# A 256-token decoder trunk on one core: two first product units interleaved by contraction tile, and transposes in two groups instead of four

## The reference

```python
for layer in range(2):
    xn = rms_norm(h, norm_mix_g[layer])
    proj = xn @ (ab_w_in, cd_w_in)[layer]
    # layer 0: causal pooling over windows 2..16, and differential attention with 6 heads
    # layer 1: gated causal convolution of width 31, and causal attention with 6 heads
    h = h + concatenate([branch_1, branch_2]) @ (ab_w_out, cd_w_out)[layer]
    hn = rms_norm(h, norm_ffn_g[layer])
    h = h + (silu(hn @ w_gate[layer]) * (hn @ w_up[layer])) @ w_down[layer]   # 1024 -> 2816 -> 1024
out = rms_norm(h, norm_final_g)
```

## Time and profile before

| what | us |
|---|---|
| median of three runs | 566.34 |
| time of the profiled execution | 566.4 |
| its span, first to last instruction | 564.1 |
| TensorE busy in the span | 556.9 (99%) |
| VectorE busy | 461.9 (82%) |
| ScalarE busy | 324.3 (57%) |
| memory read, mean rate | 104.11 MB, 186 GB/s |

### The profile page before, as it was taken

One profiled execution on the slowest core, in us unless ns is written; L12 is line 12 of the kernel. 1 busy time (PEld: TensorE's weight loads), 2 busy tenths in 40 slices (PEclk: granted clock), 3 DMA queues, 4 the chain that ended last, 5 costly groups with the idle time before them and its releaser, 6 DMA issues.

```text
span 564.1 us, 7600 instructions
## 1 busy us (share of the span) xinstructions
PE 556.9 (99%) x2949; PEld 475.1 (84%) x2949; DVE 461.9 (82%) x571; ACT 324.3 (57%) x454; POOL 15.5 (3%) x55
## 2 busy tenths in 40 slices
PE   8999999999999999999999999999999999999995
PEld 7899978888888888888888888888888888888884
DVE  5679996776988789897797998977779887798875
ACT  6686864654564555556576356546475545555543
POOL 1200001000000000000000000000000000000000
PEclk9999999999999999999999999999999999999999
DMA  8975644455627394467479622445744464926431
GB/s 297 353 298 164 217 149 145 154 195 180 223 76 243 104 314 159 145 228 255 156 242 315 226 76 74 161 146 164 273 164 140 150 223 150 304 85 215 144 112 74
DMA packets 30419, 105.65 MB, mean 187 GB/s; under 512 B 3376, under 2 KB 4272, under 8 KB 30384
## 3 DMA queue, kind: packets, MB, share of 16 engines
q1 hardware_dynamic: 30240, 105.04, 54.3%
q10 hardware_dynamic: 144, 0.14, 0.1%
HBM read 104.11 MB, written 1.05 MB: 186 GB/s over the span
## 4 chain that ended last, share of the span: by engine, by line
PE 97%; DMA 1%; issue 1%; DVE 1%; SPq 0%; ACT 0%; POOLq 0%; POOL 0%; DVEq 0%
PE bank L1748 20%; PE bank L1746 20%; PE bank L1747 20%; PE bank L2179 13%; PE bank L2182 7%; PE bank L1844 4%; PE bank L1847 2%; PE bank L1791 1%; PE bank L1795 1%; PE bank L1798 1%; PE bank L1816 1%; DMA raw<-in_slabs 1%; PE bank L1936 1%; PE bank L2224 1%; PE bank L1962 0%
## 5 line engine op out<-in xcount | busy, mean ns | idle before, releaser
L1046 DVE TENSOR_TENSOR w_lo<-raw,w_hi 128x2048 fp32r<-128x2048 f32 (+2 forms) x92 | 204.8, 2228 | 35.7 <-ACT w_hi L574 35.7
L574 ACT ACTIVATE w_hi<-raw 128x2048 fp32r<-128x2048 f32 (+2 forms) x83 | 153.7, 1862 | 28.6 <-DMA raw<-in_slabs 26.4
L1746 PE MATMUL bank<-w_lo,yT_hi 128*128 128x512 f32 (+1 forms) x242 | 96.1, 397 | 0.0
L1748 PE MATMUL bank<-w_hi,yT_lo 128*128 128x512 f32 (+1 forms) x242 | 94.1, 389 | 0.0
L1747 PE MATMUL bank<-w_hi,yT_hi 128*128 128x512 f32 (+1 forms) x242 | 94.0, 388 | 0.0
L2179 PE MATMUL bank<-xT,w_hi 128*128 128x512 f32 x320 | 80.5, 393 | 0.0
L2179 PEld LDWEIGHTS bank<-xT,w_hi 128*128 128x128 f32 x320 | 57.8, 189 | 10.6
L1746 PE MATMUL bank<-w_lo,xT 128*128 128x512 f32 (+1 forms) x160 | 61.9, 387 | 0.0
L1748 PE MATMUL bank<-w_hi,xT 128*128 128x512 f32 (+1 forms) x160 | 60.8, 380 | 0.0
L1747 PE MATMUL bank<-w_hi,xT 128*128 128x512 f32 (+1 forms) x160 | 60.6, 379 | 0.0
L1748 PEld LDWEIGHTS bank<-w_hi,yT_lo 128*128 128x128 f32 x242 | 45.4, 188 | 9.6
(11 more groups left out here) (229 smaller groups left out, 840.8 us busy)
## 6 DMA issues: line engine op xcount, KB each, us to landing
raw<-in_slabs SPq DMA_DIRECT2D x170, 512.0 KB, 4.7
spare<-in_slabs SPq DMA_DIRECT2D x16, 512.0 KB, 5.3
raw<-in_slabs SPq DMA_DIRECT2D x6, 256.0 KB, 6.1
h<-in_x SPq DMA_DIRECT2D x2, 512.0 KB, 8.6
gain<-in_norm_ffn_g SPq DMA_DIRECT2D x2, 512.0 KB, 7.2
raw<-in_slabs SPq DMA_DIRECT2D x4, 128.0 KB, 5.5
h<-in_x_cols SPq DMA_DIRECT2D x1, 512.0 KB, 6.3
gain<-in_norm_mix_g SPq DMA_DIRECT2D x1, 512.0 KB, 5.7
```

Of the source, the lines that this page charges most:

```text
L574: A(w_hi[:, s % SLOTS, c], raw_of(r, c), ACT.Copy).then_inc(hi_ready, 1)
L1046: V.tensor_tensor(w_lo[:, s % SLOTS, c], raw_of(preps[s][0], c), w_hi[:, s % SLOTS, c].bitcast(F32), ALU.subtract).then_inc(lo_ready, 1)
L1746: T.matmul(o, st_hi, mv_lo, start=first, stop=False)
L1748: return T.matmul(o, st_lo, mv_hi, start=False, stop=last)
```

## The change

There are two edits. The first interleaves the two first units: for each contraction tile `k`, TensorE does the six matmuls of unit 0 and then the six of unit 1. Slabs are renumbered to match (0: unit 0, tiles 0 to 3; 1: unit 1, tiles 0 to 3; 2: unit 0, tiles 4 to 7; 3: unit 1, tiles 4 to 7). SyncE loads the parts of slabs 0 and 1 alternately, with the token columns between them, and the last four token tiles after both slabs. ScalarE and VectorE split both slabs' parts of a tile before the next token tile; the first halves of slabs 2 and 3 are split between the token tiles 4 and 5 to 7. The copies of banks 4 and 5 wait for the third release of a slab instead of the second.

The second edit moves the turns of a seven-product unit: `turn(0)` and `turn(1)` stand together after the first contraction tile of product `t4`, and `turn(2)` and `turn(3)` together between the two blocks of the last down product. ScalarE's and VectorE's steps are reordered for it: `seven_gate(a, 1)` comes before the split of the next down slab, the split of the next up slab before `seven_hi(a, 0)`.

```diff
         SEVEN_HALF, SEVEN_CHUNK, SEVEN_TURN_BANK = (0, 1, 1, 0), (1, 1, 0, 0), (7, 4, 7, 6)
-        LAST_TURN_BANK = (7, 7, 6, 7)
+        LAST_TURN_BANK = (7, 4, 6, 7)
         EDGE = (0, 1)
...
         def part_no(s, p=0):
-            return FIRST_PARTS * s + p + 1 if s < FIRST_SLABS else FIRST_SLABS * (FIRST_PARTS - 1) + s + 1
+            return FIRST_SLABS * p + s + 1 if s < FIRST_SLABS else FIRST_SLABS * (FIRST_PARTS - 1) + s + 1
         block = ctx.enter_context(nc.Block())
...
                         .then_inc(half_loaded[n - FIRST_SLABS] if own else raw_loaded[r], 16)
-            def load_first(s):
+            def load_first():
                 for p in range(FIRST_PARTS):
                     c = slice(p * 512, (p + 1) * 512)
-                    sp.dma_start(raw[:, s, c], slabs[s, :, c]).then_inc(first_loaded[FIRST_PARTS * s + p], 16)
-                    if s == 0 and p == 0:
+                    for s in range(FIRST_SLABS):
+                        sp.dma_start(raw[:, s, c], slabs[s, :, c]).then_inc(first_loaded[FIRST_PARTS * s + p], 16)
+                    if p == 0:
                         sp.dma_start(x_rest[:, 1, :], cols_of[:, 1, :]).then_inc(cols_loaded[1], 16)
-                    if s == 0 and p == 1:
+                    if p == 1:
                         sp.dma_start(x_rest[:, 2:4, :], cols_of[:, 2:4, :]).then_inc(cols_loaded[2], 16)
-                for c0 in range(FIRST_PARTS * 512, SLAB, 256):
-                    sp.dma_start(raw[:, s, c0:c0 + 256], slabs[s, :, c0:c0 + 256]).then_inc(raw_loaded[s], 16)
-                if s == 0:
-                    sp.dma_start(x_rest[:, 4:KC, :], cols_of[:, 4:KC, :]).then_inc(cols_loaded[3], 16)
+                for s in range(FIRST_SLABS):
+                    for c0 in range(FIRST_PARTS * 512, SLAB, 256):
+                        sp.dma_start(raw[:, s, c0:c0 + 256], slabs[s, :, c0:c0 + 256]).then_inc(raw_loaded[s], 16)
+                sp.dma_start(x_rest[:, 4:KC, :], cols_of[:, 4:KC, :]).then_inc(cols_loaded[3], 16)
             def load_gain(st):
...
                     if key[1] == l and (key[0] if key[0] in ("mix", "out") else "ffn") == part:
-                        if n < FIRST_SLABS:
-                            load_first(n)
-                        else:
+                        if n == 0:
+                            load_first()
+                        elif n >= FIRST_SLABS:
                             load(n)
...
                 r, made = preps[s]
-                if FIRST_SLABS <= s < PARTED:
-                    part_his(s)
                 act.wait_ge(raw_loaded[r], made)
...
                     act.wait_ge(pow_done, pow_no("norm", 0, half))
-                    act.wait_ge(slab_used, 2)
+                    act.wait_ge(slab_used, 3)
                     A(v[:, half, 0:512], bank[:, 4 + half, :], ACT.Copy, scale=rstd[:, half:half + 1])\
...
                     seven_silu(a, 1)
+                    split_hi(up_slab(l, a + 2))
                     seven_hi(a, 0)
-                    split_hi(up_slab(l, a + 2))
+                    seven_hi(a, 1)
                     seven_silu(a, 2)
-                    seven_hi(a, 1)
-                    seven_silu(a, 3)
                     if ends_mixed(l, a):
                         split_hi(up_slab(l, a + 2) + 1)
-                        seven_hi(a, 2)
+                        seven_silu(a, 3)
                     else:
-                        seven_hi(a, 2)
+                        seven_silu(a, 3)
                         split_hi(up_slab(l, a + 2) + 1)
+                    seven_hi(a, 2)
                     seven_hi(a, 3)
...
             A(lam_t[:, 0:1], power[:, 0:1], ACT.Copy)
-            for s in range(FIRST_SLABS):
-                for p in range(FIRST_PARTS):
-                    if s or p:
-                        cols_his(4 * s + p)
-                    part_his(s, p)
-                cols_his(4 * s + FIRST_PARTS)
-                split_his(s)
+            for p in range(FIRST_PARTS):
+                if p:
+                    cols_his(p)
+                part_his(0, p)
+                part_his(1, p)
+            cols_his(3)
+            split_his(0, 1)
+            cols_his(4)
+            part_his(2)
+            cols_his(5, 6, 7)
+            part_his(3)
             split_his(2, 3)
...
             def split_lo(s):
-                if FIRST_SLABS <= s < PARTED:
-                    part_los(s)
                 dve.wait_ge(hi_ready, s + 1)
...
                     seven_add(a, 4)
+                    seven_gate(a, 1)
                     split_lo(down_slab(l, a + 1))
                     seven_act_lo(a, 0)
-                    seven_gate(a, 1)
+                    seven_act_lo(a, 1)
                     seven_add(a, 5)
...
                         seven_add(a, 6)
-                        seven_act_lo(a, 1)
                         seven_gate(a, 2)
...
                     seven_add(a, 6)
-                    seven_act_lo(a, 1)
                     seven_gate(a, 2)
...
                     seven_act_lo(a, 2)
+                    seven_act_lo(a, 3)
                     split_lo(up_slab(l, a + 2) + 1)
-                    seven_act_lo(a, 3)
                     split_lo(down_slab(l, a))
...
             V.memset(ones, 1.0).then_inc(ones_made, 1)
-            for s in range(FIRST_SLABS):
-                for p in range(FIRST_PARTS):
-                    cols_los(4 * s + p)
-                    part_los(s, p)
-                cols_los(4 * s + FIRST_PARTS)
-                split_los(s)
+            for p in range(FIRST_PARTS):
+                cols_los(p)
+                part_los(0, p)
+                part_los(1, p)
+            cols_los(3)
+            split_los(0, 1)
+            cols_los(4)
+            part_los(2)
+            cols_los(5, 6, 7)
+            part_los(3)
             split_los(2, 3)
...
                     last.then_inc(done, 1)
-            def first_unit(s, b0):
+            def first_units():
                 def split_done(parted, done, t, k):
...
                 for k in range(KC):
-                    t = s + k // 4
-                    w1, w2 = w_part(t, (k % 4) * 512, 512)
-                    if s == 0:
-                        pe.wait_ge(*((cols_hi, k) if k else (col0_hi, 1)))
-                    split_done(part_hi, hi_ready, t, k)
-                    for half in range(HALVES):
-                        T.matmul(bank[:, b0 + half, :], xT_hi[:, half, k, :], w1, start=k == 0, stop=False)
-                    if s == 0:
-                        pe.wait_ge(cols_lo, k + 1)
-                    for half in range(HALVES):
-                        T.matmul(bank[:, b0 + half, :], xT_lo[:, half, k, :], w1, start=False, stop=False)
-                    split_done(part_lo, lo_ready, t, k)
-                    for half in range(HALVES):
-                        last = T.matmul(bank[:, b0 + half, :], xT_hi[:, half, k, :], w2, start=False, stop=k == KC - 1)
-                    if k % 4 == 3:
-                        last.then_inc(slab_used, 1)
+                    for u in range(2):
+                        t, b0 = u + 2 * (k // 4), 4 + 2 * u
+                        w1, w2 = w_part(t, (k % 4) * 512, 512)
+                        if u == 0:
+                            pe.wait_ge(*((cols_hi, k) if k else (col0_hi, 1)))
+                        split_done(part_hi, hi_ready, t, k)
+                        for half in range(HALVES):
+                            T.matmul(bank[:, b0 + half, :], xT_hi[:, half, k, :], w1, start=k == 0, stop=False)
+                        if u == 0:
+                            pe.wait_ge(cols_lo, k + 1)
+                        for half in range(HALVES):
+                            T.matmul(bank[:, b0 + half, :], xT_lo[:, half, k, :], w1, start=False, stop=False)
+                        split_done(part_lo, lo_ready, t, k)
+                        for half in range(HALVES):
+                            last = T.matmul(bank[:, b0 + half, :], xT_hi[:, half, k, :], w2, start=False,
+                                            stop=k == KC - 1)
+                        if k % 4 == 3:
+                            last.then_inc(slab_used, 1)
             def rstd_rows():
...
                 if l == 0:
-                    first_unit(0, 4)
-                    first_unit(2, 6)
+                    first_units()
                 else:
...
                         down(d, 2 * i - 1, down_slab(l, d), half, half_of_acts(l, d))
-                def product(name, a, b, hi, lo):
+                def product(name, a, b, hi, lo, midway=None):
                     s, n = place[name, l, a], KC // 2
...
                     for k in range(n):
+                        if k == 1 and midway:
+                            midway()
                         w1, w2 = w_part(s, k * 512, 512)
...
                         pe.wait_ge(act_ready, U + 2 * a + j + 1)
-                        if ends_mixed(l, a) and j == 3:
```

(25 more changed lines are left out.)

## The result

The kernel after takes a median of 568.28 us (566.87 to 569.93, 8 runs), the kernel before 566.28 (565.92 to 566.49, 8 runs): the ratio is 1.004, with a 95% interval of 1.0029 to 1.0052. It is slower by 2.0 us, where 0.3 less was forecast, and lies outside the range of 565.1 to 567.2. Its runs also spread over 3.1 us, those of before over 0.6 here and over 1.3 to 1.9 in the longer rounds of the experiments. One execution of before in those rounds fell into a slow state with a lower granted clock (616.75 us, mean clock 0.85); it counts in no comparison, and all other runs are fast ones.

The account below looks back on a forecast made before the run. TensorE bounds the kernel, busy 556.9 of 564.1 us. Interleaving gains 0.2 and grouped turns 0.15, together 0.35: the profiled 566.4 becomes 566.05, the median 566.0; range 565.1 to 567.2.

Parts of the forecast that it names:

- The early start: First interleaved tiles on TensorE: third tile loses 0.27 and 0.08 us, no waits behind it, ninth tile starts at 16.7.
- I take no loss: Slab 3's load, waiting for slab 0's later split: half slab takes 4.1 us, lands 16.4 to 16.9, just inside 16.97.
- the prediction's own sum: From slab 3's landing through the splits to the first units' end: 28.1 instead of 28.31, a gain of 0.2 us.
- Rival 2: Tenth tile waits long because slab 3's first half lands later: 566.5 us, 567.5 with a later split; chance 0.10.
- 0.9 of room: Slab 5, issued about 20.5: second half lands at 25.9, low part ready 0.9 us before TensorE needs it at 31.0.
- rival 3: Slab 5, issued 2.4 us later, reaches TensorE after 31.0; landing at 27.9 costs 1.1 us: 567.1; chance 0.04.
- the copies of banks 4 and 5 at nothing: ScalarE's copies wait for the fifteenth tile, over at 26.7, but stand behind slab 5's split, so they cost nothing.
- The second edit: Grouped turns in seven-product units: seven groups vanish, saving 0.15 us, with no stall taken.
- No seven-product unit stalled: Reordered steps of the seven-product units: no stall taken; at the upper bound 0.4 us in layer 0's last unit.
- the granted clock did not fall: Groups of four transposes: clock expected to stay at 1.00; a fall would cost 3.3 us, 569.3, chance 0.01.

Follow-up runs that it names:

- run 1: First edit alone (interleaving, turns left in four groups) on the kernel before: 568.61 us, ratio 1.005 to before.
- run 4: Kernel after (both edits) with ScalarE copying banks 4 to 7 before it splits slab 6: 568.72 us, ratio 1.0043 to before.
- run 7: Kernel after (both edits) with slab 5 loaded into a raw buffer of its own: 567.04 us, ratio 1.0015 to before.
- run 3: Kernel after (both edits) with slab 3 loaded into a raw buffer of its own: 566.07 us, ratio 1.0002 to before.
- run 6: Kernel before with slab 5's load made to wait for slab 3's split as well: 566.43 us, ratio 1.0008 to before.
- run 5: Kernel after (both edits) with first halves of slabs 2 and 3 issued before the second halves: 567.43 us, ratio 1.0026 to before.
- run 2: Second edit alone on the kernel before, first units one after the other: 565.69 us, ratio 0.9996 to before.
- run 8: Kernel after plus own buffer for slab 3, first halves of slabs 2 and 3 first, slab 3's first half split before token tiles 5 to 7: 565.29 us.
- run 9: Kernel before (no interleaving) with the second edit and slab 3 in a buffer of its own: 566.02 us, ratio 0.9997 to before.
- run 10: Repeat: kernel after plus own buffer for slab 3, first halves first, slab 3's first half split before token tiles 5 to 7: 565.27 us.

## Why the prediction was wrong, step by step

**The early start: right.** No wait before the ninth tile, which started at 16.72 (16.7). That it fits so well is partly luck. The first tile began 0.32 earlier than before (4.91 for 5.23) and took 2.26 instead of 1.60, with its matmuls at half pace for longer, so that it ended 0.34 late; and the third tile's loss of 0.35 did not come.

**The step that failed: "I take no loss" for slab 3's load.** The split of slab 0 that it waits for was forecast to end at 12.7, and SyncE issued at 12.46: right. The transfer was then given 4.1 us, from a load issued into an idle queue, and a landing just inside the old 16.97. It took 5.5, to 17.93, and 5.0, 5.1 and 5.8 in runs 1, 4 and 7. The earlier trace rows was the wrong row: that load had all but an empty queue (one half slab ahead of it, which landed 0.67 after its issue), and this one was issued behind 1 MB of slab 2 still in flight. In the trace of before 33 half slabs issued with no other in flight took 3.7 to 4.5 us, and 39 issued with three others in flight 4.1 to 8.5, 6.0 at the median. There slab 3's half, issued at 10.75, had taken 6.2, landing 1.27 behind slab 2's last half, which points at its place in the queue, and not at a time of its own. The DMA view of before at that issue:

```profile
raw<-in_slabs SPq DMA_DIRECT2D x1, 512.0 KB, 6.2
```

The queue ahead does not make up the whole. In after, slab 2's last half landed at 15.99, and 1.27 behind it would be 17.26. That is 0.30 of the 0.97 by which this landing was later than before's; the other 0.67 goes with a few of its parts that landed late (below), and the cause of that stays open. Runs 1, 4 and 7 had 1.95, 1.87 and 2.83 behind slab 2's last half, runs 3 and 6, which issued earlier, 1.28 and 1.27. From the landing on the prediction's own sum goes through: ScalarE 0.96 later than 16.99, the units 0.97 later than 28.1. Rival 2 said this, from a landing after 17.3 on, and took 4.7 for it; it got a chance of 0.10, though the median of all half slabs was enough to bring it about. Its price of 566.5 to 567.5 was for this pause alone.

The Trainium skill, DMA: Bandwidth & Descriptors, "Queues, rings and completion order", states that a queue has a ring of its own on each DMA engine and that each engine takes its descriptors in ring order. The Trainium skill, DMA: Bandwidth & Descriptors, "Why a DMA increments its semaphore by 16 and not by 1", states that only the full count means that all has landed. The trace agrees with the second: the sixteen parts of this half slab landed between 15.81 and 17.93, those of slab 2's last half ahead of it between 14.05 and 15.99, and ScalarE began at 17.95, behind the last part. Twelve of the sixteen had landed by 16.35, 3.9 us after the issue, the time of a load with none ahead; the last four came at 16.76, 16.90, 17.36 and 17.93. Which engine carried which part the trace does not tell, so the ring order is not shown here.

**The second step: slab 5's "0.9 of room".** Issue 21.43 instead of 20.5, because slab 2's split slipped behind slab 3's late half on VectorE; landing 27.16 instead of 25.9; low part from 29.14:

```profile
29.14 2.29 DVE L1047 TENSOR_TENSOR w_lo<-raw,w_hi 128x2048 fp32r<-128x2048 f32 x1 [1.92 <-ACT w_hi L573]
```

It was done at 31.43, 0.5 before TensorE asked for it (29.07 and 24 matmuls of 0.12); in runs 1 and 4 TensorE had to wait 0.84 and 1.87 for it. So of the room 0.5 was left in this profile, and that only because TensorE was itself 0.97 late; in runs 1 and 4 none was. There rival 3 came along with rival 2, though they were priced as alternatives: a late slab 3 delays VectorE's split of slab 2, and by that the issue of slab 5. The chain of work that ended last in the kernel after runs through both pauses, with two transfers in it: slab 3's half from 12.46 for 5.47 us, and slab 6's second half from 25.10 for 9.11 us.

**A term that was missing.** The prediction followed slab 5 to its own matmuls and the token load to its landing, and no further. SyncE issues the residual tokens, the parameters and slab 6 behind it; ScalarE splits slab 6 ahead of the copies of banks 4 to 7; the pooling transposes wait for the last copy. I costed the copies of banks 4 and 5 at nothing because they stood behind slab 5's split. All the copies stand behind slab 6's, with 0.36 us of room before the change, and this chain cost 0.89; run 4, which puts them ahead of slab 6's split, takes that wait away.

**The second edit: right, as far as the profiles tell.** 0.15 forecast; the last matmul against the pooling transposes gave 0.15 in the kernel after and up to 0.36 in others; the runs of the second edit alone cannot tell it from nothing. No seven-product unit stalled, and the granted clock did not fall.

## What to carry to other kernels

When a reorder halves the distance between a load and its use, follow the load back to the instant it may be issued (the split that frees its buffer), and forward through the whole queue: what SyncE issues behind it is late too. Take a transfer's time from a row with the same load ahead of it, not from an idle queue, and take it as a range; where the landing decides, ask what the slowest of its parts does. A change that loses by a late buffer can win with one more buffer: here one more megabyte and two moved steps turned 2.0 us lost into 0.9 gained.

## What the runs showed of the hardware

- The same half slab of 512 KB took 3.8 us from issue to landing in run 5 (behind half of slab 2), 5.0 to 5.8 in runs 1, 4 and 7 and the kernel after (behind all of it), 6.2 in the kernel before, issued 1.7 us earlier, and in run 3, issued four microseconds earlier, 8.3. From the DMA view of run 3:

```profile
extra<-in_slabs SPq DMA_DIRECT2D x1, 512.0 KB, 8.3
```

- A packet of 4 KB took 159 ns at the median. Between 14 and 18 us 34 of some 310 packets of the kernel after took over 300 ns, up to 1160; in runs 1, 4 and 7 there were 27 to 37 such, in before and runs 2, 5 and 6 15 to 20 of some 345, and in runs 3, 8, 9 and 10, whose slab 3 was queued right behind slab 2 by 9.5 us, at most 1 of some 400. So the slow packets went along with the late landings. That is a correlation; what makes these packets slow is not settled.
- The first matmuls of 512 columns start 0.43 us apart instead of 0.227, about half pace, and for how long differs between profiles of the same instructions: in before the first pair only, in the kernel after until 6.33 us, in run 2 until 6.91. The first six took 1.62 us in before, 2.26 in after and 2.34 in run 2, where 1.36 is the full pace. The trace's record of the granted clock begins, at 1.00 (2.4 GHz), at 5.57 in before, 6.62 in after and 6.97 in run 2, just where the pace changes; for the matmuls ahead of it it has no value. No run changed this.
